# Two-block float32 kernel: the first gate's mixing with the token values stationary, and its row sums as two rounded products

## The chip, the cores and the metric

One core of one Trainium2 chip runs the whole program. The metric is the device time of one execution in microseconds, taken as the median of several runs. The compute engines are TensorE (matrix products, PE in the profile; PEld is its loading of the stationary operand), VectorE (DVE), ScalarE (ACT) and GpSimd (POOL); SyncE (SP) issues most DMAs.

## The reference, cut to what matters

The kernel computes two transformer blocks for 512 tokens of width 1024. The change lies in the spatial gate of the first block (`gmlp_mixer`), with 16 heads of 128 channels and groups of 128 tokens:

```python
u, v, z = jnp.split(h @ w_in, 3, axis=-1)          # each 512 x 2048
u = jax.nn.gelu(u)
v = layer_norm(jax.nn.gelu(v), ln_g, ln_b)
vg = v.reshape(bsz, s // 128, 128, 16, 128)
w_m = jnp.where(allowed[None], w_s, 0)             # per head 128 x 128, s-chunks up to t's
mixed = jnp.einsum('hts,bgshc->bgthc', w_m, vg)
mixed = mixed + b_s.T[:, :, None]
y = u * mixed.reshape(bsz, s, 2048) * jax.nn.silu(z)
return y @ w_out
```

The layer norm's gain `ln_g` and shift `ln_b` are per channel, so the kernel applies them behind the mixing: mixed = ln_g * (W n) + ln_b * (row sums of W) + b_s, where n is the normalised v without gain and shift.

## The kernel before

All matrix products are made of float32 operands split into two rounded parts (`hi`, and `lo` = value - `hi`, type fp32r): a product is `mm3`, three TensorE products hi*hi, lo*hi and hi*lo (L499 to L501) that accumulate in PSUM. Every weight comes in slabs of 128x1024 in one global order: SyncE loads a slab into `raw`, ScalarE rounds it into `whi` (a "cut", L1079), GpSimd subtracts to get `wlo` (L489), and TensorE uses it; the ring has four places, so the cut of a slab waits until TensorE has used the slab four places before. `slab()` is one slab on TensorE: 8 x 3 products of 512 columns into one PSUM bank.

In front of the gate, v has been computed token-major into `vraw` (tokens in partitions, 2048 channels). The gate then runs in eight rounds i, each with two heads q = 0, 1. A round takes four slabs "uz": 4i and 4i+1 give u of the two heads (banks 0 and 1), 4i+2 and 4i+3 give z (banks 2 and 3), all channel-major (channels in partitions, 512 tokens in columns). In round 0 slab 2 comes ahead of the mixing. Beside that, in each round:

- VectorE normalises the round's 256 channels of `vraw` (`norm`, L1629), ScalarE rounds them into `vhi` (L1140) and VectorE makes `vlo` (L1633). ScalarE rounds the two heads' mixing matrices `wt` (s in partitions, t in columns, 128x128 each) into `wthi` (L1143), and VectorE makes `wtlo` (L1636).
- TensorE sums the columns of `wt` over the partitions with a float32 product with `ones` into bank 3 (`rows`, L586, between slabs 4i and 4i+1), and VectorE makes of it the two heads' rows of `bb` = ln_b * rows + b_s (L1641).
- After slab 4i+1 TensorE mixes: `mm3` with `wthi`/`wtlo` stationary and the values moving, 512 columns, into bank 4+q (`mix`, L596). The result is token-major. ScalarE copies it to `mt` (`mixed`, L1157), TensorE transposes it in four 128x128 pieces into bank 6+q (`turn`, L607), after slab 4i+2 for q = 0 and after slab 4i+3 for q = 1.
- VectorE makes mt = ln_g * turned + bb (`affine`, L1647), times gelu(u) (`gate`, L1654), times silu(z) (`y`, L1657), and splits it into `yhi`, `ylo` (L1660, L1662), first all for q = 0, then all for q = 1. ScalarE makes gelu(u) (`u0`, `u1`, L1146, L1153) and silu(z) (`z0`, `z1`, L1159, L1161).

Each engine executes its own list in order. Between engines the order is set by semaphores, counted by `Steps`: `X.at("name", i)` is the count at which step "name" of round i is done. VectorE's list in a round is norm, vlo, wlo, bb, then affine, gate, y, yhi, ylo for q = 0 and for q = 1; norm of round i+1 waits for ylo1 of round i. ScalarE's is cut, vhi, whi, cut, u0, two small loads of the next `wt`, cut, u1, mixed0, mixed1, cut, z0, z1. Behind the gate the output projection `w1` begins.

## Time and profile before

| | |
|---|---|
| median of 3 runs | 1323.53 us (1321.55 to 1324.12) |
| profiled execution, time | 1324.05 us |
| its span, first to last instruction | 1322.3 us |
| TensorE busy | 1303.1 us (99%), 6515 products |
| VectorE busy | 728.6 us (55%) |
| ScalarE busy | 664.7 us (50%) |
| GpSimd busy | 497.0 us (38%) |
| mean granted TensorE clock | 0.994 of full speed |

A timeline gives for each instruction its start and length in us from the start of the span. TensorE's products are pipelined: one is recorded from its start to its last result, and the next starts before that, so cost is read from the distance between starts. A row with "x4" merges four instructions, from the first start to the last end. In brackets stands how long the engine was idle before it, and what released it. "L586" is a line of the kernel.

### The profile page before, as it was taken

How to read it: one execution, taken by the hardware profiler on the slowest of the kernel's cores; microseconds unless marked ns; L12 is line 12 of the kernel's file. 1: busy time of each engine (PE TensorE's matmuls, PEld its weight loads, DVE VectorE, ACT ScalarE, POOL GpSimd, SP SyncE). 2: the span in 40 equal slices, each digit the busy share in tenths (PEclk: the TensorE clock that was granted, in tenths of full speed). 3: DMA queues.
4: the chain of work that ended last, by engine and by line, in shares of the span. 5: the costliest groups of instructions: out<-in, count | busy, mean ns of one | idle time of the engine just before them, and what ended most of it. 6: DMA issues, size and time to landing. Idle time of an engine off the chain costs nothing.

```text
span 1322.3 us, 16669 instructions
## 1 busy us (share of the span) xinstructions
PE 1303.1 (99%) x6515; PEld 1089.8 (82%) x6515; DVE 728.6 (55%) x1288; ACT 664.7 (50%) x999; POOL 497.0 (38%) x207
## 2 busy tenths in 40 slices
PE   9999999999999999999999999999999999999997
PEld 7888888888887788888878888888878888888896
DVE  5556466462137465565865467666645556643444
ACT  5535444443234567575547566656545545552321
POOL 4543433434444322321436433433333333334520
PEclk9999999999999999999999999999999999999998
DMA  5732322324333222322243322222223222235411
GB/s 182 266 119 83 102 84 83 102 83 160 96 111 96 82 92 71 113 68 63 84 154 110 96 65 65 79 80 64 80 81 98 75 81 84 86 106 173 153 39 65
DMA packets 43455, 131.31 MB, mean 99 GB/s; under 512 B 7088, under 2 KB 11888, under 8 KB 42864
## 3 DMA queue, kind: packets, MB, share of 16 engines
q1 hardware_dynamic: 38144, 116.41, 28.5%
q10 hardware_dynamic: 5232, 13.83, 3.0%
q8 instruction: 52, 0.85, 0.3%
q14 instruction: 27, 0.22, 0.1%
HBM read 123.92 MB, written 10.49 MB: 102 GB/s over the span
## 4 chain that ended last, share of the span: by engine, by line
PE 80%; DVE 10%; ACT 6%; issue 2%; DMA 1%; POOL 1%; SPq 0%; DVEq 0%; ACTq 0%
PE banks L499 24%; PE banks L501 24%; PE banks L500 24%; PE banks L685 2%; DVE hd L1899 1%; PE banks L677 1%; PE banks L666 1%; DMA raw<-w 1%; DVE naccb L1804 1%; DVE ylo L1701 1%; ACT L1344 1%; ACT L1343 1%; PE banks L910 1%; PE banks L791 1%; DVE nfull L1697 1%
## 5 line engine op out<-in xcount | busy, mean ns | idle before, releaser
L489 POOL TENSOR_TENSOR wlo<-raw,whi 128x1024 fp32r<-128x1024 f32 (+2 forms) x198 | 486.0, 2456 | 744.8 <-ACT whi L1079 744.5
L499 PE MATMUL banks<-hhi,whi 128*128 128x512 f32 x752 | 307.0, 408 | 2.4 <-DVE hlo L1831 1.2
L501 PE MATMUL banks<-hlo,whi 128*128 128x512 f32 x752 | 294.7, 392 | 0.0
L500 PE MATMUL banks<-hhi,wlo 128*128 128x512 f32 x752 | 294.1, 391 | 0.0
L1079 ACT ACTIVATE whi<-raw 128x1024 fp32r<-128x1024 f32 (+2 forms) x198 | 205.6, 1039 | 173.5 <-PE banks L501 109.4
L499 PE MATMUL banks<-yhi,whi 128*128 128x512 f32 x448 | 176.9, 395 | 0.2 <-DVE ylo L1701 0.2
L501 PE MATMUL banks<-ylo,whi 128*128 128x512 f32 x448 | 174.7, 390 | 0.0
L500 PE MATMUL banks<-yhi,wlo 128*128 128x512 f32 x448 | 174.4, 389 | 0.0
L499 PEld LDWEIGHTS banks<-hhi,whi 128*128 128x128 f32 x752 | 142.0, 189 | 32.1 <-issue 3.1
L501 PEld LDWEIGHTS banks<-hlo,whi 128*128 128x128 f32 x752 | 141.4, 188 | 30.7
L500 PEld LDWEIGHTS banks<-hhi,wlo 128*128 128x128 f32 x752 | 142.1, 189 | 27.1 <-issue 2.2
L499 PEld LDWEIGHTS banks<-yhi,whi 128*128 128x128 f32 x448 | 84.1, 188 | 20.9 <-issue 3.2
L501 PEld LDWEIGHTS banks<-ylo,whi 128*128 128x128 f32 x448 | 84.1, 188 | 18.0
L500 PEld LDWEIGHTS banks<-yhi,wlo 128*128 128x128 f32 x448 | 84.1, 188 | 17.3 <-issue 0.2
L499 PE MATMUL banks<-whi,yhi 128*128 128x512 f32 x224 | 89.3, 399 | 0.7 <-DVE ylo L1559 0.7
L500 PE MATMUL banks<-whi,ylo 128*128 128x512 f32 x224 | 87.9, 392 | 0.0
L501 PE MATMUL banks<-wlo,yhi 128*128 128x512 f32 x224 | 87.8, 392 | 0.0
L499 PEld LDWEIGHTS banks<-whi,yhi 128*128 128x128 f32 x224 | 42.4, 189 | 11.6 <-issue 1.4
L1647 DVE SCALAR_TENSOR_TENSOR mt<-banks,vec,bb 128x512 f32<-128x512 f32 x16 | 12.0, 751 | 70.2 <-PE banks L607 70.2
L500 PEld LDWEIGHTS banks<-whi,ylo 128*128 128x128 f32 x224 | 42.4, 189 | 9.0 <-issue 0.5
L501 PEld LDWEIGHTS banks<-wlo,yhi 128*128 128x128 f32 x224 | 42.5, 190 | 8.9
L1216 ACT ACTIVATE sc<-sc,sm 128x128 f32<-128x128 f32 (+1 forms) x64 | 35.2, 552 | 27.5 <-DVE sm L1759 27.5
(385 smaller groups left out, 2212.9 us busy)
## 6 DMA issues: line engine op xcount, KB each, us to landing
raw<-w SPq DMA_DIRECT2D x193, 512.0 KB, 3.6
rel_tab<-relx ACTq DMA_DIRECT2D x1, 4096.0 KB, 20.3
tab<-rel_tab SPq DMA_DIRECT2D x16, 224.0 KB, 3.5
x<-xt ACTq DMA_DIRECT2D x1, 2048.0 KB, 9.4
x_kept<-x ACTq DMA_DIRECT2D x1, 2048.0 KB, 7.3
parts_kept<-mcg SPq DMA_DIRECT2D x8, 256.0 KB, 4.4
mgt<-parts_kept SPq DMA_DIRECT2D x8, 256.0 KB, 4.1
x<-x_kept ACTq DMA_DIRECT2D x1, 2048.0 KB, 7.9
```

The lines of the kernel that those rows point to most:

```text
L489: nc.gpsimd.tensor_tensor(lo[:, begin:width], raw[:, n % 2, begin:width], f32(hi[:, begin:width]), ALU.subtract).then_inc(lo_done, 1)
L499: nc.tensor.matmul(dst, a[0], b[0], start=first, stop=False)
L500: nc.tensor.matmul(dst, a[1], b[0], start=False, stop=False)
L501: return nc.tensor.matmul(dst, a[0], b[1], start=False, stop=last)
L666: done = nc.tensor.matmul(banks[:, c:c + QW[t]], a[rows, t * P:(t + 1) * P], b[rows, 0:QW[t]], start=first, stop=last)
L677: last = nc.tensor.transpose(banks[:, c:c + P], sc[:, q, of:of + P], ident)
L685: last = nc.tensor.matmul(bank[AO[i][q]][:, k * P:S], av[q][:, i, k, :], p[:, q, AK[q][k]:AK[q][k] + KW[k]], start=k == 0 and p is phi, st ...
L791: nc.tensor.matmul(bank[6], ones, ho[:, 0, :], start=True, stop=True).then_inc(hoP.did("ms"), 1)
L910: last = nc.tensor.transpose(bank[b][:, c:c + P], msc[:, QO[t] + k * P:QO[t] + (k + 1) * P], ident)
L1079: nc.scalar.activation(parts(slab)[0][:, begin:width], raw[:, n % 2, begin:width], ACT.Copy).then_inc(hi_done, 1)
L1216: e = nc.scalar.activation(row, row, ACT.Exp, bias=sm[:, q, 1, t:t + 1], accum_out=sm[:, q, 2, t:t + 1])
L1343: nc.scalar.activation(he[:, :], bank[0], ACT.Sigmoid).then_inc(hpA.did("f"), 1)
```

## The change

Mixing is turned round. The stationary operand is now a 128x128 tile of the values (`vhi` or `vlo`; tokens of one tile t by the channels of head q), and the moving one is the head's matrix: the two parts of it lie side by side in one tile `wts[:, q, g, :]` (g = 0 hi, g = 1 lo). For each head and token tile there are two products: `vhi` with both parts (256 columns, start), and `vlo` with the hi part (128 columns), which accumulates onto the first half. The result is channel-major, so nothing is transposed. It lies in two PSUM banks per head (`mixes[q]`), with vhi*hi + vlo*hi in half 0 and vhi*lo in half 1 of each token tile. ScalarE copies half 1, times ln_g, to `mt` (`mixed`), VectorE adds ln_g times half 0 (`affine`), and a further VectorE step adds `bb` (`shift`).

The row sums are now two products of 256 columns with a rounded `rones` stationary, over the hi and over the lo parts of the two heads. They stand behind slab 4i+1 and behind the wait for `wlo`, directly ahead of the mixing. `rones` is made once by VectorE. ScalarE no longer waits for `rows` ahead of the loads of the next `wt`, and TensorE no longer waits for these loads itself.

```diff
--- before.py
+++ after.py
@@ -203,8 +203,8 @@
             vhi = sb("vhi", [P, TT, 2 * P], F32R, scope)
             vlo = sb("vlo", [P, TT, 2 * P], F32R, scope)
             wt = sb("wt", [P, 2, P], F32, scope)
-            wthi = sb("wthi", [P, 2, P], F32R, scope)
-            wtlo = sb("wtlo", [P, 2, P], F32R, scope)
+            wts = sb("wts", [P, 2, 2, P], F32R, scope)
+            rones = sb("rones", [P, P], F32R, scope)
             mt = sb("mt", [P, 2, S], F32, scope)
             ug = sb("ug", [P, 2, S], F32, scope)
             sz = sb("sz", [P, 2, S], F32, scope)
@@ -285,6 +285,7 @@
 
         banks = ctx.enter_context(nc.psum_tensor("banks", [P, 8 * S], F32))
         bank = [banks[:, i * S:(i + 1) * S] for i in range(8)]
+        mixes = [banks[:, (4 + 2 * q) * S:(6 + 2 * q) * S].rearrange("p (t g v) -> p t g v", t=TT, v=P) for q in range(2)]
 
 
 
@@ -339,11 +340,11 @@
         vA = steps("v_act", numbered("gelu", TT), 4)
         vV = steps("v_dve", numbered("stats", TT), 4)
         vaA = steps("va_act", ["root"])
-        vaV = steps("va_dve", ["mask", "aggr", "eps", "inv", "shift"])
-        uzP = steps("uz_pe", ["rows", "mix0", "mix1", "turn0", "turn1"], 8, prime=1)
+        vaV = steps("va_dve", ["mask", "ones", "aggr", "eps", "inv", "shift"])
+        uzP = steps("uz_pe", ["rows", "mix0", "mix1"], 8, prime=1)
         uzA = steps("uz_act", ["vhi", "whi", "u0", "u1", "mixed0", "mixed1", "z0", "z1"], 8, prime=1)
         uzV = steps("uz_dve", ["norm", "vlo", "wlo", "bb"] + [f"{n}{q}" for q in range(2)
-                    for n in ("affine", "gate", "y", "yhi", "ylo")], 8, prime=1)
+                    for n in ("affine", "shift", "gate", "y", "yhi", "ylo")], 8, prime=1)
         w1A = steps("w1_act", ["sq", "hi"], KT)
         w1V = steps("w1_dve", ["x", "acc", "lo"], KT)
         avP = steps("av_pe", numbered("v", TT - 1), 2)
@@ -578,35 +579,30 @@
                     pe.wait_ge(vA.sem, vA.at(f"gelu{TT - 1}", 2))
                 pe.wait_ge(uzA.sem, uzA.at("u0", i - 1))
                 slab("uz", 4 * i, bank[0], h)
-                pe.wait_ge(uzA.sem, uzA.at("z1", i - 1))
-                pe.wait_ge(ld_wt, 32 * i + 32)
-                if i == 0:
-                    pe.wait_ge(vaV.sem, vaV.at("mask"))
-                    pe.wait_ge(vA.sem, vA.at(f"gelu{TT - 1}", 2))
-                nc.tensor.matmul(bank[3][:, 0:2 * P], ones, wt[:, :, :], start=True, stop=True).then_inc(uzP.did("rows"), 1)
                 pe.wait_ge(uzA.sem, uzA.at("u1", i - 1))
                 slab("uz", 4 * i + 1, bank[1], h)
                 if i == 0:
                     slab("uz", 2, bank[2], h)
                     pe.wait_ge(vA.sem, vA.all())
                 pe.wait_ge(uzV.sem, uzV.at("wlo", i))
+                pe.wait_ge(uzA.sem, uzA.at("z1", i - 1))
+                for g in range(2):
+                    rows = nc.tensor.matmul(bank[3][:, 0:2 * P], rones[:, :], wts[:, :, g, :], start=g == 0, stop=g == 1)
+                rows.then_inc(uzP.did("rows"), 1)
                 for q in range(2):
-                    pe.wait_ge(uzA.sem, uzA.at(f"mixed{q}", i - 1))
+                    pe.wait_ge(uzV.sem, uzV.at(f"affine{q}", i - 1))
                     cols = slice(q * P, (q + 1) * P)
-                    mm3(bank[4 + q][:, :], (wthi[:, q, :], wtlo[:, q, :]), (vhi[:, :, cols], vlo[:, :, cols]),
-                        True, True).then_inc(uzP.did(f"mix{q}"), 1)
+                    for t in range(TT):
+                        nc.tensor.matmul(mixes[q][:, t, :, :], vhi[:, t, cols], wts[:, q, :, :], start=True, stop=False)
+                        mix = nc.tensor.matmul(mixes[q][:, t, 0, :], vlo[:, t, cols], wts[:, q, 0, :], start=False,
+                                               stop=True)
+                    mix.then_inc(uzP.did(f"mix{q}"), 1)
                 for q in range(2):
                     if i or q:
                         pe.wait_ge(uzA.sem, uzA.at(f"z{q}", i - 1))
                         if q == 1:
                             pe.wait_ge(uzV.sem, uzV.at("bb", i))
                         slab("uz", 4 * i + 2 + q, bank[2 + q], h)
-                    pe.wait_ge(uzA.sem, uzA.at(f"mixed{q}", i))
-                    pe.wait_ge(uzV.sem, uzV.at(f"affine{q}", i - 1))
-                    for t in range(TT):
-                        turn = nc.tensor.transpose(bank[6 + q][:, t * P:(t + 1) * P], mt[:, q, t * P:(t + 1) * P],
-                                                   ident)
-                    turn.then_inc(uzP.did(f"turn{q}"), 1)
 
 
             pe.wait_ge(uzA.sem, uzA.at("u0", 7))
@@ -1140,12 +1136,11 @@
                 nc.scalar.activation(vhi[:, :, :], vraw[:, :, bass.ds(i * 2 * P, 2 * P)],
                                      ACT.Copy).then_inc(uzA.did("vhi"), 1)
                 act.wait_ge(ld_wt, 32 * i + 32)
-                nc.scalar.activation(wthi[:, :, :], wt[:, :, :], ACT.Copy).then_inc(uzA.did("whi"), 1)
+                nc.scalar.activation(wts[:, :, 0, :], wt[:, :, :], ACT.Copy).then_inc(uzA.did("whi"), 1)
                 cut()
                 act.wait_ge(uzV.sem, uzV.at("gate0", i - 1))
                 nc.scalar.activation(ug[:, 0, :], bank[0][:, :], ACT.Gelu_apprx_tanh).then_inc(uzA.did("u0"), 1)
                 act.wait_ge(uzV.sem, uzV.at("wlo", i))
-                act.wait_ge(uzP.sem, uzP.at("rows", i))
                 act.dma_start(wt[0:64, :, :], ws[0:64, bass.ds(2 * i + 2, 2), :]).then_inc(ld_wt, 16)
                 act.dma_start(wt[64:P, :, 64:P], ws[64:P, bass.ds(2 * i + 2, 2), 64:P]).then_inc(ld_wt, 16)
                 cut()
@@ -1154,7 +1149,8 @@
                 for q in range(2):
                     act.wait_ge(uzP.sem, uzP.at(f"mix{q}", i))
                     act.wait_ge(uzV.sem, uzV.at(f"ylo{q}", i - 1))
-                    nc.scalar.activation(mt[:, q, :], bank[4 + q][:, :], ACT.Copy).then_inc(uzA.did(f"mixed{q}"), 1)
+                    nc.scalar.activation(mt[:, q, :].rearrange("p (t v) -> p t v", v=P), mixes[q][:, :, 1, :], ACT.Copy,
+                                         scale=col("ln_g", 2 * i + q)).then_inc(uzA.did(f"mixed{q}"), 1)
                 cut()
                 nc.scalar.activation(sz[:, 0, :], bank[2][:, :], ACT.Silu).then_inc(uzA.did("z0"), 1)
                 used("uz", 4 * i + 3)
@@ -1608,6 +1604,7 @@
                 if k in (2, 6):
                     stats_of(1 if k == 2 else 2)
             stats_of(3)
+            V.tensor_copy(rones[:, :], ones).then_inc(vaV.did("ones"), 1)
             dve.wait_ge(vV.sem, vV.all())
             for t in range(TT):
                 last = V.bn_aggr(mv[:, t, :], stats[:, t, :, :])
@@ -1633,7 +1630,7 @@
                 V.tensor_tensor(vlo[:, :, :], vraw[:, :, bass.ds(i * 2 * P, 2 * P)], f32(vhi[:, :, :]),
                                 ALU.subtract).then_inc(uzV.did("vlo"), 1)
                 dve.wait_ge(uzA.sem, uzA.at("whi", i))
-                V.tensor_tensor(wtlo[:, :, :], wt[:, :, :], f32(wthi[:, :, :]), ALU.subtract).then_inc(uzV.did("wlo"), 1)
+                V.tensor_tensor(wts[:, :, 1, :], wt[:, :, :], f32(wts[:, :, 0, :]), ALU.subtract).then_inc(uzV.did("wlo"), 1)
                 if i == 0:
                     dve.wait_ge(ld_bs, 16)
                 dve.wait_ge(uzP.sem, uzP.at("rows", i))
@@ -1643,13 +1640,14 @@
                 last.then_inc(uzV.did("bb"), 1)
                 dve.wait_ge(uzV.sem, uzV.at("bb", i))
                 for q in range(2):
-                    dve.wait_ge(uzP.sem, uzP.at(f"turn{q}", i))
-                    V.scalar_tensor_tensor(mt[:, q, :].rearrange("p (t v) -> p t v", v=P),
-                                           bank[6 + q][:, :].rearrange("p (t v) -> p t v", v=P),
-                                           col("ln_g", 2 * i + q),
-                                           bb[:, bass.ds(2 * i + q, 1), :].to_broadcast([P, TT, P]),
-                                           ALU.mult, ALU.add).then_inc(uzV.did(f"affine{q}"), 1)
+                    dve.wait_ge(uzA.sem, uzA.at(f"mixed{q}", i))
+                    mt3 = mt[:, q, :].rearrange("p (t v) -> p t v", v=P)
+                    V.scalar_tensor_tensor(mt3, mixes[q][:, :, 0, :], col("ln_g", 2 * i + q), mt3, ALU.mult,
+                                           ALU.add).then_inc(uzV.did(f"affine{q}"), 1)
                     dve.wait_ge(uzV.sem, uzV.at(f"affine{q}", i))
+                    V.tensor_tensor(mt3, mt3, bb[:, bass.ds(2 * i + q, 1), :].to_broadcast([P, TT, P]),
+                                    ALU.add).then_inc(uzV.did(f"shift{q}"), 1)
+                    dve.wait_ge(uzV.sem, uzV.at(f"shift{q}", i))
                     dve.wait_ge(uzA.sem, uzA.at(f"u{q}", i))
                     V.tensor_tensor(mt[:, q, :], mt[:, q, :], ug[:, q, :], ALU.mult).then_inc(uzV.did(f"gate{q}"), 1)
                     dve.wait_ge(uzV.sem, uzV.at(f"gate{q}", i))
```

## Rows read from the trace of the kernel before

**Rows 1.** The page: busy time of each engine, and the chain that ended last.

```profile
PE 1303.1 (99%) x6515; PEld 1089.8 (82%) x6515; DVE 728.6 (55%) x1288; ACT 664.7 (50%) x999; POOL 497.0 (38%) x207
...
PE 80%; DVE 10%; ACT 6%; issue 2%; DMA 1%; POOL 1%; SPq 0%; DVEq 0%; ACTq 0%
```

**Rows 2.** Work by stretch (us, then busy us of each engine, clock, DMA): the first gate.

```profile
97.65:294.90 197.25, 197.25 (x898) 162.53 (x897) 112.58 (x150) 93.53 (x118) 79.92 (x32) 1.00 0.30 91
```

**Rows 3.** TensorE's timeline (start us, length us), round 3 of the gate.

```profile
201.76 0.60 PE L586 MATMUL banks<-wt,cst 128*128 128x256 f32 x2
...
202.43 0.39 PE L500 MATMUL banks<-hhi,wlo 128*128 128x512 f32 x1
...
207.68 0.40 PE L499 MATMUL banks<-vhi,wthi 128*128 128x512 f32 x1
...
209.07 0.39 PE L499 MATMUL banks<-hhi,whi 128*128 128x512 f32 x1
...
214.56 0.60 PE L607 MATMUL banks<-cst,mt 128*128 128x128 f32 x4
...
215.22 0.39 PE L500 MATMUL banks<-hhi,wlo 128*128 128x512 f32 x1
...
220.46 0.60 PE L607 MATMUL banks<-cst,mt 128*128 128x128 f32 x4
...
232.29 0.40 PE L499 MATMUL banks<-vhi,wthi 128*128 128x512 f32 x1
```

**Rows 4.** TensorE's timeline, first and last of 23 products, 256 columns.

```profile
1011.06 0.28 PE L500 MATMUL banks<-whi,llo 128*128 128x256 f32 x1
...
1013.70 0.28 PE L501 MATMUL banks<-wlo,lhi 128*128 128x256 f32 x1
```

**Rows 5.** TensorE's timeline, second block: 128-column products, then one of 512.

```profile
732.67 0.22 PE L499 MATMUL banks<-hqxhi,hkhi 128*128 128x128 f32 x1
...
733.57 0.39 PE L500 MATMUL banks<-hhi,wlo 128*128 128x512 f32 x1
```

**Rows 6.** TensorE's timeline, round 0 of the gate.

```profile
115.61 0.40 PE L501 MATMUL banks<-vlo,wthi 128*128 128x512 f32 x1
116.01 0.66 PE L607 MATMUL banks<-cst,mt 128*128 128x128 f32 x4
```

**Rows 7.** VectorE's timeline: rounds 0 and 3, then behind the gate.

```profile
108.41 0.42 DVE L1636 TENSOR_TENSOR wtlo<-wt,wthi 128x256 fp32r<-128x256 f32 x1
...
117.56 0.69 DVE L1654 TENSOR_TENSOR mt<-mt,ug 128x512 f32<-128x512 f32 x1
...
215.26 0.75 DVE L1647 SCALAR_TENSOR_TENSOR mt<-banks,vec,bb 128x512 f32<-128x512 f32 x1 [8.62 <-PE banks L607]
216.05 2.85 DVE L1654 TENSOR_TENSOR mt<-mt,ug 128x512 f32<-128x512 f32 x1
...
222.61 2.77 DVE L1657 TENSOR_TENSOR mt<-mt,sz 128x512 f32<-128x512 f32 x1
...
230.33 0.42 DVE L1636 TENSOR_TENSOR wtlo<-wt,wthi 128x256 fp32r<-128x256 f32 x1
230.66 0.61 DVE L1641 SCALAR_TENSOR_TENSOR bb<-banks,vec,bb 128x128 f32<-128x128 f32 x2
...
307.81 0.69 DVE L1673 TENSOR_TENSOR x<-x,banks 128x512 f32<-128x512 f32 x1 [9.22 <-DMA x<-xt]
```

**Rows 8.** GpSimd's timeline, round 3 and the start of round 4.

```profile
215.96 2.40 POOL L489 TENSOR_TENSOR wlo<-raw,whi 128x1024 fp32r<-128x1024 f32 x1 [4.46 <-ACT whi L1079]
222.29 2.54 POOL L489 TENSOR_TENSOR wlo<-raw,whi 128x1024 fp32r<-128x1024 f32 x1 [3.94 <-ACT whi L1079]
230.41 2.60 POOL L489 TENSOR_TENSOR wlo<-raw,whi 128x1024 fp32r<-128x1024 f32 x1 [5.58 <-ACT whi L1079]
```

**Rows 9.** ScalarE's timeline, round 3: the first silu.

```profile
217.19 0.60 ACT L1159 ACTIVATE sz<-banks 128x512 f32<-128x512 f32 x1
```

**Rows 10.** GpSimd's timeline, round 0.

```profile
117.67 2.84 POOL L489 TENSOR_TENSOR wlo<-raw,whi 128x1024 fp32r<-128x1024 f32 x1 [3.36 <-ACT whi L1079]
```

## What the change will do to the time

> **What bounds the kernel now.** I read the page first. TensorE is busy for 1303.1 of 1322.3 us, and the chain that ended last is 80% TensorE work [rows 1]. That alone says little, since a busy share is an average over stages, so I then read the three stretches: before, inside and after the first gate. In the gate (97.65 to 294.90 us, the eight rounds that the change edits) TensorE is busy for 197.25 of 197.25 us, while VectorE has 112.6, ScalarE 93.5 and GpSimd 79.9 us of work; the granted clock is 1.00, the upper of the two levels (2.4 GHz) [rows 2]. So in this stretch time is what TensorE has to issue, and every us taken from it is worth a us, as long as nothing else becomes late. The reader should see both halves: the sum of TensorE's work, and the slack of the chain that feeds it.
>
> For the sum I don't take durations, which overlap (a 512-column product lasts 0.39 us, yet the next starts 0.23 us later), but distances between starts, in one steady round (round 3) of TensorE's timeline [rows 3].
>
> **What TensorE loses, per round.** The row sum over `ones` (L586, float32, two passes): from its start at 201.76 to 202.43, the second product after it, is 0.67, less one usual distance of 0.23, so 0.44 us. Mixing: six products of 512 columns, 207.68 to 209.07, 1.39 us. Transposes: four at 214.56, and 215.22 - 214.56 - 0.23 = 0.43 us; the group at 220.46 is its twin, so 0.86 us. Together 2.69 us [rows 3].
>
> **What TensorE gains, per round.** Rows: two rounded products of 256 columns. Back-to-back products of that width and type stand 2.64 us apart over 22 steps, 0.120 us each [rows 4], so 0.24 us. Mixing: for each of two heads and four token tiles one product of 256 columns and one of 128. For 128 columns the trace has the hgrn products: six of them from 732.67, then wide ones, of which the second starts at 733.57; 0.90 less 0.23 is 0.67 us, 0.111 each [rows 5]. One pair thus costs 0.231 and eight pairs 1.85 us. I take 0.120 after the wide one and 0.111 after the narrow one because each distance is measured in a series of its own width; no row shows them alternating. Bounds: both at 0.111 give 1.78 us, both at 0.120 give 1.92 us. The columns streamed are the same as before (6x512 = 8x384 = 3072), so the stationary reloads cost 0.46 us per round, and what is won is the transposes and the cheaper row sum. New total 2.09 us, a gain of 0.60 us per round (0.53 to 0.67), 4.8 us in eight rounds (4.2 to 5.4).
>
> A rule that would change this term: the Trainium skill, TensorE: Matmul & The Clock Gate, section Back-to-back issue gap, gives the isolated distance at the full clock as N/2.4 + 2.5 ns, that is 56 ns for 128 columns. An estimate by that page makes new mixing 8x(0.109+0.056) = 1.32 us and the total gain some 4 us larger. The row of 0.111 us disagrees, so I price by the row; the same page's LDWEIGHTS section (128 columns, about 107 ns) agrees with the row.
>
> One idle piece goes as well: in round 0 TensorE's last mixing product starts at 115.61, its successor could start at 115.84, and the transposes start at 116.01 because they wait for ScalarE's copy [rows 6]. That is 0.17 us, once. The new order has no such wait; what stands in its place is `bb`, which slab 3 waits for. `bb` starts after `rows`, which is now ahead of 1.85 us of mixing, and takes 0.61 us of VectorE [rows 7]: covered.
>
> **What moves, and who waits.** The rows' product moves from behind slab 4i to behind slab 4i+1, and now waits for `wlo` and, with it, the mixing. Queued behind it on TensorE is everything. So the question is whether `wlo` still comes in time. ScalarE loses its wait on `rows` ahead of the two small `wt` loads; that wait was long over, and both loads are issued from the same place. VectorE's `bb` is later by one slab (5.49 us), but VectorE then sat idle for 8.62 us waiting for the transposes [rows 7], so nothing queues behind it that matters. ScalarE's copy out of PSUM gets a scale and a strided source; even at twice its time it is hidden, since what it starts (affine0, shift0, gate0) is done some 5 us before z0, which y0 needs as well. One extra 128x128 copy (`rones`) lies in VectorE's prologue, where `wlo` of round 0 ends at 108.83 [rows 7] and the last of six mixing products starts at 115.61 [rows 6], so some 5 us are free; without that cover it would cost 0.2 us once.
>
> **The chain that feeds TensorE.** It is z1 and y0, then affine1, gate1, y1, yhi1, ylo1, norm, vhi, vlo, `wlo`. Measured from the end of slab 4i+3 (220.46, where the twin of the transposes starts): `wlo` ends at 230.33 + 0.42 = 230.75 [rows 7], 10.29 us later; mixing starts at 232.29 [rows 3], 11.83 later. Slack 1.54 us. After the change TensorE asks for `rows` after two slabs only, 2 x 5.49 = 10.98 us, and VectorE has one more instruction per head, `shift`, a 128x512 sum of two SBUF tensors (0.69 us, like the gate at 117.56 [rows 7]). Naively 10.29 + 0.72 = 11.01 and the slack is gone. But the row to look at is y1 itself: 2.77 us instead of 0.69, from 222.61 to 225.38. GpSimd runs its split from 222.29 to 224.83 [rows 7, 8]. Gate0 shows the same (2.85 us, ending 218.90, 0.54 after GpSimd's 218.36). VectorE's sums of two SBUF tensors stand still while GpSimd works, and end 0.54 us after it. Y1's end is pinned to GpSimd, and part of the new instruction fits in the time it stood.
>
> The Trainium skill, SBUF — State Buffer, section SBUF: two separate sides, states this as an exclusive lock: whichever of a two-SBUF-input VectorE instruction and a GpSimd instruction starts first holds it to its end. The trace agrees.
>
> Worked through in the clock of round 3 (slab 4i+2 ends at 214.56): mixing no longer waits for transposes, so affine0, shift0 and gate0 run early, shift0 behind a GpSimd split, done some 5 us after `rows`, far ahead of z0 (217.19 + 0.60 = 217.79 [rows 9]). Y0 then stands until 218.90; yhi0 and ylo0 end at 220.09, affine1 (0.75) at 220.88, shift1 at 221.61, gate1 runs 221.64 to 222.33. Slab 4i+3 ends at 214.56 + 5.49 = 220.05 and GpSimd's split asks 1.83 us later (222.29 - 220.46), at 221.88, 0.24 after gate1 began. It then ends 2.26 us after the VectorE instruction that held it up, as at 117.67 + 2.84 = 120.51 against 117.56 + 0.69 [rows 7, 10], at 224.59, and y1 at 225.13: 5.08 after the slab, where it was 4.92. So `wlo` is done 10.45 us after the slab and TensorE asks at 10.98. Slack 0.53 us, no stall. If gate1 loses the race, y1 ends at 225.54, `wlo` at 10.86: still in time. Round 0 is out of step (no slab 2 between mixing and slab 3): there ylo0 ends near 122.2, shift1 holds off GpSimd, gate1 stands behind it, and `wlo` of round 1 ends 132.6 against a request at 132.6: a stall of 0.1 us, 0.7 if shift1 loses.
>
> **The sum.** 4.8 + 0.17 - 0.1 = 4.9 us. Behind the gate all is paced by TensorE or relative to it; the load of `x`, issued when ylo1 of round 7 is done, lands for 307.81 [rows 7], and TensorE needs that sum four slabs after 294.7, at 316.7, so it is hidden as before. The profiled execution took 1324.05 us (span 1322.3), so 1319.2; it stood 0.5 above the median of the three runs, so the median would be 1318.7. I say 1319.0.
>
> **Rivals.** (A) VectorE's chain becomes the bound. If shift1 loses to GpSimd too (needs affine1 0.95 us later than worked out), `wlo` comes 10.86 + 0.72 = 11.58 after the slab, 0.60 us late in seven rounds, 4.2 us: 1323.4, no change. For: slack falls from 1.54 to 0.53 us. Against: the pin to GpSimd. Chance 0.10. (B) Slower: `wlo` starts at 230.33, GpSimd's next split at 230.41 [rows 7, 8], 0.08 us apart. Should the split start first, in every round, because ScalarE's `whi` into the interleaved tile is that much quicker or `vlo` later, `wlo` ends near 230.41 + 2.40 + 0.27 = 233.08, about 12.8 us after the slab with the 0.16 from above, 1.8 us late seven times: 1324.05 - 5.0 + 12.6 = 1331.7. It decides at 0.08 us. Against: both hang on the same `vhi`, and the eight pairs of the eight rounds all stand 0.08 to 0.10 apart. Chance 0.06. (C) A narrow product costs its columns only. From 0.229 us for 512 (5.49 over 24) and 0.120 for 256 columns [rows 3, 4], a straight line gives 0.066 for 128: a pair 0.186, mixing 1.49 us, 8 x 0.36 = 2.9 us more gain, 1316.3. Against: the series at 0.111 [rows 5], though in it every product is narrow and reloads follow each other at once, where here a wide one stands between. Chance 0.04; it is the side to which the page's formula points. The forecast has 0.80.
>
> **Numbers.** A measurement of this kernel can tell about 0.2% (2.6 us) from no change. Low end: best bounds 5.4 + 0.17 off 1324.05 give 1318.5, less 0.5 for the median and 1.7 for scatter (the runs shown spread 2.6): 1316.3, which takes in C as well. High end takes in A, 1323.4. B stays out, with the tails of the rest. Forecast and C are faster (0.83 after a little for scatter), A is within 0.2%, some of it with B: same 0.11, slower 0.06.
>
> **What the profile after would show.** No transposes; products of 256 and 128 columns with starts 0.120 and 0.111 apart; a round of 24.0 us instead of 24.62; TensorE without idle time in the gate except at most 0.1 us ahead of `rows` of round 1; shift0 near 3 us long, shift1 0.69; y1 ending about 5.1 us after slab 4i+3; `wlo` 0.42 long ending 0.5 us before `rows`. What would make me wrong: TensorE waiting for `wlo` in each round (A for 0.6, B for 1.8 us with a long `wlo`), or other distances between the short products.

## The result, and the profile after

The changed kernel took 1314.7 us in the median of five runs (1314.39 to 1315.8), the kernel before 1323.53 beside it (1321.53 to 1324.48): ratio 0.994, 95% interval 0.9928 to 0.9952. It is faster by 8.8 us, where 4.5 to 4.9 were forecast; 1314.7 lies 1.6 us under the low end of the range. Two later series of the same two kernels gave 1315.59 against 1322.94 (0.9939) and 1315.45 against 1323.62 (0.994). The profiled execution took 1314.39 us, span 1312.6.

The page of the kernel after (busy time of each engine; chain that ended last), beside [rows 1]:

```profile
PE 1295.1 (99%) x6531; PEld 1087.0 (83%) x6531; DVE 729.9 (56%) x1305; ACT 664.4 (51%) x999; POOL 496.0 (38%) x207
...
PE 80%; DVE 11%; ACT 6%; issue 2%; POOL 0%; DMA 0%; DVEq 0%; SPq 0%; ACTq 0%
```

Nothing changed its role. To find where 9.7 us of span went I cut both spans at the same events: the first column sum behind the gate's projection, the second group of mean squares, what follows it, and TensorE's last products. Windows of the kernel before (us; busy us of PE, PEld, DVE, ACT, POOL; granted clock; DMA share; GB/s), then of the kernel after:

```profile
384.50:674.30 289.80, 287.13 (x1496) 238.54 (x1494) 179.47 (x397) 172.88 (x301) 99.16 (x41) 1.00 0.29 91
674.30:682.30 8.00, 8.00 (x33) 6.60 (x34) 1.70 (x7) 1.16 (x2) 2.39 (x1) 0.79 0.42 147
682.30:1314.50 632.20, 625.20 (x3288) 530.59 (x3287) 356.92 (x640) 324.77 (x484) 229.59 (x93) 1.00 0.28 87
1314.50:1322.30 7.80, 0.67 (x2) 0.00 (x0) 3.22 (x8) 0.00 (x0) 0.00 (x0) 0.50 0.41 136
```

```profile
97.65:290.00 192.35, 192.30 (x919) 161.74 (x918) 113.73 (x168) 94.26 (x118) 80.06 (x32) 1.00 0.32 94
...
378.50:668.30 289.80, 287.10 (x1496) 238.55 (x1494) 179.43 (x397) 172.63 (x301) 99.17 (x41) 1.00 0.30 91
668.30:674.70 6.40, 6.40 (x34) 5.47 (x34) 1.71 (x7) 1.16 (x2) 2.39 (x1) 1.00 0.38 153
674.70:1306.10 631.40, 625.00 (x3288) 530.43 (x3287) 358.01 (x640) 324.37 (x484) 228.99 (x93) 1.00 0.29 88
1306.10:1312.60 6.50, 0.41 (x2) 0.00 (x1) 3.22 (x8) 0.00 (x0) 0.00 (x0) 0.54 0.49 161
```

The reader should see separate pieces. Up to the column sum the kernel after is 6.0 us ahead (384.5 against 378.5). Over the next 290 us the two differ by some 0.02 us. Then 1.6 us come in a stretch of 8 us where the clock column reads 0.79 against 1.00, 0.8 us over the long rest, and 1.3 us in the last 8 us. So 3.7 us of the 9.7 lie where nothing was edited. The 0.8 us lie within the scatter: the same rest takes 632.2 and 633.0 us in the two profiles of the kernel before, and 631.4, 632.5 and 632.6 in the three of the kernel after.

The time in front of the gate is no constant either, so the edited part is best measured between two events of its own: the gate's first product and the column sum. TensorE's timeline, kernel before, then after:

```profile
97.65 0.39 PE L499 MATMUL banks<-hhi,whi 128*128 128x512 f32 x1
...
384.53 0.61 PE L649 MATMUL banks<-cst,nacc 128*128 128x1 f32 x5
```

```profile
97.56 0.39 PE L500 MATMUL banks<-hhi,whi 128*128 128x512 f32 x1
...
378.53 0.61 PE L645 MATMUL banks<-cst,nacc 128*128 128x1 f32 x5
```

That is 286.88 against 280.97 us, a gain of 5.9. Every profile of either kernel gives these two lengths within 0.01 us; "later" and "earlier" below are differences between such lengths.

In the gate, TensorE's timeline of round 3 of the kernel after (start us, length us), beside [rows 3]:

```profile
204.20 0.40 PE L590 MATMUL banks<-wts,rones 128*128 128x256 f32 x2
204.44 0.28 PE L596 MATMUL banks<-wts,vhi 128*128 128x256 f32 x1
204.56 0.22 PE L597 MATMUL banks<-wts,vlo 128*128 128x128 f32 x1
204.62 0.33 PE L596 MATMUL banks<-wts,vhi 128*128 128x256 f32 x1
204.79 0.22 PE L597 MATMUL banks<-wts,vlo 128*128 128x128 f32 x1
...
206.24 0.44 PE L500 MATMUL banks<-hhi,whi 128*128 128x512 f32 x1
206.52 0.40 PE L501 MATMUL banks<-hhi,wlo 128*128 128x512 f32 x1
...
228.06 0.40 PE L590 MATMUL banks<-wts,rones 128*128 128x256 f32 x2
```

From the rows to the second wide product, less one distance: 206.52 - 204.20 - 0.23 = 2.09 us, as forecast. A pair (204.79 less 204.56) is 0.23, but not split as forecast: 0.06 us pass from the narrow product to the wide one behind it (204.62) and 0.17 from that to the next. The round, though, is 228.06 - 204.20 = 23.86 us, where 24.0 was forecast. The kernel before has its next row sum at 226.37, a round of 24.61:

```profile
226.37 0.60 PE L586 MATMUL banks<-wt,cst 128*128 128x256 f32 x2
```

Take the short work away from both: 24.61 - 2.69 = 21.92 us for the four slabs of a round before, 23.86 - 2.09 = 21.77 after. The same 96 wide products cost 0.2283 us each before and 0.2268 after. That is 0.15 us a round, 1.2 us in eight.

The chain that feeds TensorE, in VectorE's timeline of the kernel after, and GpSimd's beside it:

```profile
208.09 1.07 DVE L1648 TENSOR_TENSOR mt<-mt,bb 128x512 f32<-128x512 f32 x1
...
218.69 0.69 DVE L1652 TENSOR_TENSOR mt<-mt,ug 128x512 f32<-128x512 f32 x1
219.42 2.77 DVE L1655 TENSOR_TENSOR mt<-mt,sz 128x512 f32<-128x512 f32 x1
...
227.13 0.42 DVE L1633 TENSOR_TENSOR wts<-wt,wts 128x256 fp32r<-128x256 f32 x1
```

```profile
219.00 2.62 POOL L490 TENSOR_TENSOR wlo<-raw,whi 128x1024 fp32r<-128x1024 f32 x1 [3.47 <-ACT whi L1075]
227.22 2.58 POOL L490 TENSOR_TENSOR wlo<-raw,whi 128x1024 fp32r<-128x1024 f32 x1 [5.59 <-ACT whi L1075]
```

Gate1 starts ahead of GpSimd's split (218.69 against 219.00), y1 is stretched and ends at 222.19, and `wlo` ends at 227.55, 0.51 us ahead of the rows at 228.06. Forecast was 0.53.

### The profile page after: what moved, and what is told of

The parts are those of the page before. It is cut to its first block, busy times and chain, and to the rows that moved or that the text cites. A ratio compares the mean times of both kernels' runs of the same rounds, so it can differ in the third digit from the quotient of the medians.

```text
span 1312.6 us, 16685 instructions
## 1 busy us (share of the span) xinstructions
PE 1295.1 (99%) x6531; PEld 1087.0 (83%) x6531; DVE 729.9 (56%) x1305; ACT 664.4 (51%) x999; POOL 496.0 (38%) x207
## 4 chain that ended last, share of the span: by engine, by line
PE 80%; DVE 11%; ACT 6%; issue 2%; POOL 0%; DMA 0%; DVEq 0%; SPq 0%; ACTq 0%
PE banks L500 24%; PE banks L502 24%; PE banks L501 24%; PE banks L681 2%; DVE hd L1897 1%; PE banks L673 1%; PE banks L662 1%; DVE naccb L1802 1%; DVE ylo L1699 1%; PE banks L596 1%; ACT L1340 1%; ACT L1339 1%; PE banks L906 1%; PE banks L787 1%; DVE hb L1894 1%
## 5 line engine op out<-in xcount | busy, mean ns | idle before, releaser
L1655 DVE TENSOR_TENSOR mt<-mt,sz 128x512 f32<-128x512 f32 x16 | 26.3, 1642 | 37.8 <-ACT sz L1155 37.5
```

The lines of the kernel that those rows point to most:

```text
L1655: V.tensor_tensor(mt[:, q, :], mt[:, q, :], sz[:, q, :], ALU.mult).then_inc(uzV.did(f"y{q}"), 1)
```

## The experiments

**Both kernels again.** The spread and the landmarks have to be known before parts are compared.

> The kernel before, unchanged: how far one execution stands from another. The gate (first product at 97.65, first of the column-wise sums behind the output projection at 384.5) should repeat within 0.2 us. Theory G (the difference between the two profiled executions is 6.0 us in the gate and the rest is which level the clock happened to be at): the stretch at 1.2 GHz that the first profile had behind the mean squares (675 to 679 us, 1.5 us lost) is there in some executions and not in others, and the span varies by 1 to 3 us. Theory R (the rest of the gain belongs to the change): the stretch is there again at the same place, and the median stays near 1323.5.

> The changed kernel, unchanged. Theory G: the gate repeats (sums behind the projection at 378.5), and the stretch behind the mean squares may be at 1.2 GHz this time, which costs 1.5 us; over many executions the mean difference to before should come out nearer to 6 to 7 us than to 9. Theory R: no low clock there, difference 8.8 again.

Measured: before 1323.04 us (0.9998, 0.9989 to 1.0007), column sum at 384.4; after 1315.59 (0.9939, 0.9926 to 0.9953), column sum at 378.4. So the 6.0 us come back to a tenth. I also counted in the two traces, up to the column sum, the wide products whose distance to the next is above 0.2285 us ("slow" from here on), and summed their excess over 0.2267: 249 and 1.43 us before, 23 and 0.10 us after. The 1.6 us behind the mean squares don't come back: this profile of the kernel before has the full clock there and a span of 1321.2.

**The parts of the gate.** The new rows alone, in the kernel before:

```diff
-                nc.tensor.matmul(bank[3][:, 0:2 * P], ones, wt[:, :, :], start=True, stop=True).then_inc(uzP.did("rows"), 1)
...
+                for g, part in enumerate((wthi, wtlo)):
+                    rows = nc.tensor.matmul(bank[3][:, 0:2 * P], rones[:, :], part[:, :, :], start=g == 0, stop=g == 1)
```

> The kernel before with the row sums alone changed (two rounded products directly ahead of the mixing; mixing and transposes as before). By the prediction's prices the sums behind the projection come 8 x 0.20 = 1.6 us earlier (at 382.9). Theory S (each interruption of a series of 512-column products makes the next 5 to 16 of them slower, 0.227 to 0.231 us): 8 x 0.04 more, 1.9 us, and 512-column products slower than 0.2285 us fall from 240 to about 170 in the gate. Time 1321.6 to 1321.9.

Measured: 1318.45 us (0.9968, 0.9955 to 0.998), column sum at 382.3, 2.1 us earlier, and 168 slow products (0.96 us) in place of 249. A round is 24.36 us, 0.25 shorter where the prices give 0.20.

The kernel before without its transposes:

```diff
-                    for t in range(TT):
-                        turn = nc.tensor.transpose(bank[6 + q][:, t * P:(t + 1) * P], mt[:, q, t * P:(t + 1) * P],
-                                                   ident)
...
-                                           bank[6 + q][:, :].rearrange("p (t v) -> p t v", v=P),
+                                           bank[4 + q][:, :].rearrange("p (t v) -> p t v", v=P),
```

> The kernel before without the transposes: the affine step reads the token-major mixing result as if it were channel-major, so this part of the result is not computed as in the reference. By the prediction's prices 8 x 0.86 + 0.17 = 7.05 us less up to the sums behind the projection (377.5). Theory S: another 8 x 0.045, 7.4 us (377.1), and some 80 slow 512-column products fewer in the gate. The chain to wlo gets no longer than before plus nothing, as no shift step is added: TensorE is not idle in the gate.

Measured: 1315.57 us (0.9944, 0.9932 to 0.9957), 170 slow products (1.00 us). The column sum is at 377.4, which looks like 7.0 us, just what the prices alone give. But TensorE had waited 1.1 us for a cut of ScalarE's in front of the gate, where the kernels do not differ, and the gate began late. Its first product and the column sum:

```profile
98.21 0.39 PE L499 MATMUL banks<-hhi,whi 128*128 128x512 f32 x1
...
377.41 0.61 PE L643 MATMUL banks<-cst,nacc 128*128 128x1 f32 x5
```

That is 279.20 us, 7.7 less than before; theory S had 7.4. A round is 23.68 us, 0.93 shorter where the prices give 0.86.

The changed kernel with the float32 row sum back in its old place:

```diff
+                nc.tensor.matmul(bank[3][:, 0:2 * P], ones, wt[:, :, :], start=True, stop=True).then_inc(uzP.did("rows"), 1)
...
-                for g in range(2):
-                    rows = nc.tensor.matmul(bank[3][:, 0:2 * P], rones[:, :], wts[:, :, g, :], start=g == 0, stop=g == 1)
```

> The changed kernel with the row sums undone (float32 product at its old place between slabs 4i and 4i+1, mixing new). By the prices: the sums behind the projection 1.6 us later than in the changed kernel (380.1). Theory S: 1.6 + 8 x 0.04 = 1.9 us later (380.4), with 9 slow 512-column products behind each of the eight.

Measured: 1317.63 us (0.9964, 0.9951 to 0.9977), column sum at 380.2, 1.7 us later than after, between the 1.6 of the prices and the 1.9 of theory S; 86 slow products (0.48 us). By the counts the float32 row sum leaves 8 to 10 slow products behind it each time ((249 - 168)/8, (86 - 24)/8), a group of four transposes about 5 ((249 - 170)/16), and old mixing about 11 (the rest, 249 - 81 - 79 = 89 in eight rounds), five of its own six among them (the six took 1.39/6 = 0.232 us each). The new mixing and rows leave at most 3 a round.

**Interruptions elsewhere.** Four products of 128 columns ahead of a slab in six rounds of the projection behind the gate, in the changed kernel, once as float32 transposes and once on rounded operands:

```diff
+                if m >= 2:
+                    for t in range(TT):
+                        nc.tensor.transpose(bank[5][:, t * P:(t + 1) * P], ident, ident)
```

```diff
+                if m >= 2:
+                    for t in range(TT):
+                        nc.tensor.matmul(bank[5][:, t * P:(t + 1) * P], yhi[:, 0, 0:P], yhi[:, 0, 0:P], start=True, stop=True)
```

> The changed kernel with four extra 128x128 float32 transposes of the identity into an unused bank in each of six output-projection rounds (between the two slabs, m from 2): 24 in all, nothing else. Own cost 6 x 0.43 = 2.6 us. Theory S: five or more slow 512-column products behind each group, 6 x 0.025 = 0.15 us more; in the changed kernel this stretch has 3 slow ones, here it should have over 30.

> The changed kernel with four products of 128 columns on rounded (fp32r) operands in each of the last six projection rounds, where the run with four float32 transposes there (e8) came out at the column sum behind the projection 3.0 us later than the changed kernel and with 37 more slow 512-column products (0.23 us). Here the four cost 4 x 0.056 to 4 x 0.111 us a round (the narrow product of a wide and narrow pair, at most), 1.3 to 2.7 us in all. Theory F (only float32 products leave slow 512-column products behind them): the number of slow products stays near the changed kernel's 24 (0.09 us); column sum at 379.8 to 381.1. Theory I (any interruption of the stream does): 30 to 40 slow products more and 0.2 us, column sum at 380.0 to 381.4. The count tells them apart, the time does not.

Measured: transposes 1319.69 us (0.9982, 0.9973 to 0.9991), column sum at 381.5, 2.9 us later, 61 slow products (0.34 us): 6 a group. Rounded products 1319.23 us (0.9964, 0.995 to 0.9977), column sum at 381.4, 2.8 us later, 33 slow products (0.15 us): 1.5 a group. So the count went theory F's way; the time did not, 381.4 being later than F's 381.1. TensorE's timeline of the rounded ones shows why:

```profile
338.79 0.56 PE L619 MATMUL banks<-yhi 128*128 128x128 f32 x4
339.19 0.45 PE L500 MATMUL banks<-yhi,whi 128*128 128x512 f32 x1
339.47 0.40 PE L501 MATMUL banks<-yhi,wlo 128*128 128x512 f32 x1
```

The four take 339.19 - 338.79 = 0.40 us, but the wide product behind them is followed after 0.28 us instead of 0.23, 0.45 us in all, six times 2.7. Old mixing ran on rounded operands too and was slow, so "float32 only" is not the whole rule: a group of short rounded products is cheap to interrupt with, a float32 group is not. What in the engine makes the next five to ten products 2 to 9 ns late stays open.

**How much slack the chain has.** One, then two more sums of two SBUF tensors between shift1 and gate1 of each round, in the changed kernel:

```diff
+                    if q == 1:
+                        V.tensor_tensor(spare[:, :], ug[:, q, :], sz[:, 0, :], ALU.add).then_inc(uzV.did("more0"), 1)
```

> The changed kernel with one more 128x512 sum of two SBUF tensors per round on VectorE, into a spare tile, between shift1 and gate1 (0.72 us with its start). The slack of the chain to wlo is 0.51 us in the changed kernel. Naive theory (each VectorE instruction counts in full): wlo 0.2 us late in seven rounds, 1.5 us. Theory P (y1 is pinned to the end of GpSimd's split): the extra sum holds the split off or gate1 stands behind it; y1 ends at most 0.4 us later, no more than 0.1 us idle in a round beyond round 1, time within 0.5 us of the changed kernel.

> Two such sums (1.44 us). Naive theory: wlo 0.93 us late in seven rounds, 6.5 us. Theory P: the first 0.7 us vanish against GpSimd's split; one sum is held up by it and what is behind comes after: 0.5 to 0.7 us idle ahead of the rows' product in seven rounds, 3.5 to 4.9 us slower than the changed kernel.

Measured: one sum 1318.07 us (0.9965, 0.9953 to 0.9978), column sum at 381.5, 3.0 us later; two 1322.65 us (1.0001, 0.9991 to 1.001), at 385.9, 7.2 us later. Theory P had 0.5 us at most and 3.5 to 4.9, the naive one 1.5 and 6.5, so the idea of the prediction that time in this chain is hidden behind y1's pin to GpSimd falls. VectorE's timeline with one sum more:

```profile
220.56 0.69 DVE L1654 TENSOR_TENSOR spare<-ug,sz 128x512 f32<-128x512 f32 x1
221.16 2.88 DVE L1655 TENSOR_TENSOR mt<-mt,ug 128x512 f32<-128x512 f32 x1
224.08 0.69 DVE L1658 TENSOR_TENSOR mt<-mt,sz 128x512 f32<-128x512 f32 x1
```

Now gate1 is the one that stands while GpSimd works, and y1 runs behind it in 0.69: one stretched instruction has taken the other's place and everything behind is 0.72 us later. TensorE's timeline with one sum (first fence) and with two:

```profile
205.43 0.39 PE L503 MATMUL banks<-hlo,whi 128*128 128x512 f32 x1
205.92 0.50 PE L591 MATMUL banks<-wts,rones 128*128 128x256 f32 x2
206.26 0.28 PE L597 MATMUL banks<-wts,vhi 128*128 128x256 f32 x1
```

```profile
207.45 0.39 PE L503 MATMUL banks<-hlo,whi 128*128 128x512 f32 x1
208.55 0.50 PE L591 MATMUL banks<-wts,rones 128*128 128x256 f32 x2 [0.71 <-DVE wts L1634]
```

The rows come 0.49 and 1.10 us after the last wide product, where 0.23 is usual: 0.26 and 0.87 us of waiting, for 0.72 and 1.44 us of added work. So the slack was 0.46 to 0.57 us, which is what the timeline showed (0.51), and the naive theory has the waits right (0.2 and 0.93). A wait costs more than its length: the rows then take 0.34 us instead of 0.24, and with some more slow products behind them (43 in the trace with one sum, against 23) a steady round loses 0.41 us instead of 0.26.

**The end of the kernel.** A window over the last DMA issues, kernel before and then after (packets of each queue; last line: issues and median us to landing):

```profile
q1 hardware_dynamic: 345, 0.30, 32.4%
q14 instruction: 1, 0.01, 0.7%
...
out<-x SPq DMA_DIRECT2D x1, 128.0 KB, 2.8
```

```profile
q1 hardware_dynamic: 647, 0.58, 60.5%
...
out<-x SPq DMA_DIRECT2D x3, 128.0 KB, 1.8
```

In the kernel before a load of instructions (8 KB, queue q14) starts 2.16 us ahead of the end of the span, in the midst of the last output packets. All but 15 of these have started by 1.75 us ahead of the end; those 15 follow one at a time until 0.85 us ahead of it. From VectorE's last end to the end of the span it is 3.8 us there and 2.8 in the kernel after, whose load starts 14.4 us ahead of the end. Every kernel with the small copy into `rones` has the short end, every one without it the long one. So I added that tile and its copy to the kernel before, and the tile alone:

```diff
+            rones = sb("rones", [P, P], F32R, scope)
...
+            V.tensor_copy(rones[:, :], ones).then_inc(vaV.did("ones"), 1)
```

> The kernel before with one addition, the tile of rounded ones and the one VectorE copy that fills it, which nothing reads. Every profile of a kernel without that copy (before, its repeat, the one without transposes) has an 8 KB instruction load on queue q14 2.2 to 2.3 us ahead of the end of the span, the last output DMA taking 2.8 us to land, and 3.7 to 3.8 us from VectorE's last end to the end of the span; every profile with the copy has that load 11 us or more ahead of the end, a landing of 1.8 us and 2.8 us from VectorE's end. Theory L (where the instruction load falls depends on how many instructions VectorE has in its program, and it holds up one DMA engine at the end): with the copy the load moves away from the end, the last landing is 1.8 us, VectorE's end to the span's end 2.8 us, and the median is 0.9 to 1.1 us below the kernel before: 1321.6 to 1322.1; the gate is unchanged (column sum behind the projection at 384.4 to 384.6, some 249 slow products). Rival N (the short tail comes from something else that the new rows or the new mixing bring): the load stays 2.2 us ahead of the end, the tail is 3.8 us, the median 1322.5 to 1323.1.

> The kernel before with the tile of rounded ones declared and nothing done with it: the tiles behind it in the gate's part of the memory shift by 512 bytes per partition, no instruction is added. Theory L (the count of VectorE's instructions places the load): nothing changes, load 2.2 to 2.4 us ahead of the end, tail 3.7 to 3.8 us, median 1322.5 to 1323.1. Rival M (the layout of the memory shortens the tail): tail 2.8 us, median 1321.6 to 1322.1. If the slow 512-column products hung on the layout too, their number in the gate would fall from some 249; by what they follow it stays.

Measured: with the copy 1321.98 us (0.9989, 0.9981 to 0.9998), with the tile alone 1322.78 (0.9999, 0.999 to 1.0008). The same window of the two, copy first:

```profile
q1 hardware_dynamic: 654, 0.59, 61.2%
...
out<-x SPq DMA_DIRECT2D x3, 128.0 KB, 1.8
```

```profile
q14 instruction: 1, 0.01, 1.0%
...
out<-x SPq DMA_DIRECT2D x1, 128.0 KB, 2.6
```

With the copy the load has moved to 11.6 us ahead of the end, and the tail is 2.8 us; with the tile alone it is at 2.25 us and the tail is 3.6. Both gates are unchanged (249 slow products, column sum at 384.6 and 384.3). One instruction more in VectorE's program thus takes about a microsecond off the end (0.8 us between the two medians, 1.3 against the kernel before, interval of the latter 0.3 to 2.5), in a place that has nothing to do with it. Theory L's forecast came. The other profiles agree: the load starts 2.2 to 2.3 us ahead of the end in all four with 1288 VectorE instructions, 11.2 and 11.6 in the two with 1289, 14.1 to 14.9 in the six with 1305, 17.5 with 1313 (one sum more) and 23.5 with 1321 (two), whether TensorE has 6451 or 6555 products. So its place follows VectorE's number of instructions. That it holds up one DMA engine fits the rows but was not shown.

**The clock.** The 1.6 us behind the mean squares:

> The changed kernel once more, for the share of the gain that the granted clock has. Of 58 runs of the kernel before, 17 had a mean granted clock of 0.994 (mean 1323.9 us), 16 of 0.995 (1322.9), 22 of 0.996 (1322.15) and 3 of 0.997; of the 10 runs of the changed kernel so far, one had 0.995 and nine 0.996 or 0.997 (eight at 0.996, mean 1315.1 us). At equal clock the gain is 7.0 us, which is 6.0 us of the gate and 1.0 us of the last landing; what the medians show above that would be the clock. Theory K (the changed kernel falls to the lower clock less often): at least 8 in 10 of the runs at 0.996 or more, median 1314.5 to 1315.6. Rival Z (it was the draw of ten runs): about half of the runs at 0.994 or 0.995, median 1315.6 to 1316.5, and the gain over the kernel before 7.0 us or a little more.

Measured: 1315.45 us (0.994, 0.9926 to 0.9953); mean clocks 0.996 four times and 0.997 once, where six of the nine runs of the kernel before beside it had 0.994 or 0.995. With the earlier ones that is 14 of 15 runs of the changed kernel at 0.996 or more, and 28 of 67 of the kernel before. Theory K holds as an observation. TensorE's timeline of the kernel before shows what one such stretch is:

```profile
673.38 1.02 PE L751 MATMUL banks<-cst,nacc 128*128 128x1 f32 x8 [0.30 <-DVE naccb L1804]
674.27 1.03 PE L751 MATMUL banks<-cst,naccb 128*128 128x1 f32 x8
675.16 0.65 PE L499 MATMUL banks<-whi,yhi 128*128 128x512 f32 x1
675.61 0.63 PE L500 MATMUL banks<-whi,ylo 128*128 128x512 f32 x1
676.03 0.63 PE L501 MATMUL banks<-wlo,yhi 128*128 128x512 f32 x1
```

Behind sixteen products of one column, from 675.3 to 678.7, wide products last 0.63 us and start 0.43 apart: the granted clock is at its lower level (1.2 GHz) and costs 1.6 us. In the profiles of the kernel after, three in all, the same sixteen products are followed by the upper level. Of the kernel before one has it and one hasn't. But four variants of the changed kernel have it in their profiles (the old row sum, one and two more sums, the added transposes), and with the added transposes 6 of 10 runs had a mean clock of 0.994 or 0.995. So the runs don't tie the upper level to the change itself. Why the changed kernel falls less often is open; two identical executions can differ in it. This third profile of the kernel after has its column sum at 379.1, 0.6 us later than the first, all of it from in front of the gate (first product at 98.11); its gate is as long as the others'.

## Why the prediction was wrong

**TensorE bounds the gate**: right. 192.30 of 192.35 us busy, as [rows 2].

**Removed 2.69, added 2.09 us per round**: right to a hundredth, but in the sum only. The distances inside a pair were 0.17 and 0.06 us and not the 0.120 and 0.111 that the prediction said the profile would show. The narrow product handed on after 0.06 us, a quarter of the 0.227 of 512 columns, and the wide one took the difference back. The prediction had said that no row shows the two alternating; that its sum held to a hundredth is in part luck. The pair cost 0.231 and not 0.186, so rival C's gain did not come. The isolated distance that the Trainium skill gives (TensorE: Matmul & The Clock Gate, section Back-to-back issue gap), 56 ns for 128 columns, fits the narrow product's 0.06 us; as a price of the pair (0.165 us, an estimate by that page) it does not.

**"Slab 5.49 us", the step that failed inside the gate.** I read a slab's length once, [rows 3], with its slow products in it, and held it constant. It is no constant: it carries the after-effect of what interrupts the stream. Taking away the float32 rows, the transposes and old mixing made the 96 wide products of a round 0.15 us shorter: 0.05 by the row sum and 0.07 by the transposes (the rounds of e3 and e4 against the prices), the rest by old mixing. The term was missing from the sum and measured 1.2 us.

**Idle time 0.17 and the stall of 0.1**: the stall of round 1 was longer. TensorE's timeline of the kernel after:

```profile
132.07 0.39 PE L502 MATMUL banks<-hlo,whi 128*128 128x512 f32 x1
132.51 0.51 PE L590 MATMUL banks<-wts,rones 128*128 128x256 f32 x2
132.85 0.29 PE L596 MATMUL banks<-wts,vhi 128*128 128x256 f32 x1
```

The rows come 0.44 us after the last wide product, a stall of 0.21, and take 0.34 instead of 0.24, so this pair comes to 0.17 - 0.31 = -0.14 instead of +0.07. The sum for the gate is 4.8 + 1.2 - 0.14 = 5.9, and 5.9 was measured.

**The chain, rival A and rival B**: the forecast of 0.53 us of slack was right (0.51); neither rival came. `wlo` still starts 0.09 us ahead of the split (B's margin was 0.08). But the reason I gave against A was too good: e6 and e7 show that one instruction more would have brought A's waiting. Shift0 was 1.07 us long and not near 3, as GpSimd's split had begun 1.9 us earlier; nothing hung on it.

**"Behind the gate all is paced by TensorE or relative to it", the second step that failed.** It held for the arithmetic (289.80 us both), not for the instruction load at the end (1.0 us in the profiles) nor for the clock. At an equal mean clock of 0.996 the kernel before averages 1322.2 us (24 runs) and the kernel after 1315.3 (12 runs): 6.9 us, which is the gate's 5.9 and the end's 1.0. What the medians of the three series show above that, 0.5 to 1.9 us, goes with the clock and with scatter; the runs don't separate the two.

So the direction was right and so was what bounds the gate, and 3.9 us of the 8.8 were not in the sum of 4.9: 1.0 in the gate, 1.0 at the end, and 1.9 of clock and scatter. Without these 1.9 the median would have been 1316.6, just inside the range; the range had 1.7 us for scatter, but only on top of the best bounds of the terms that the sum had.

## What to carry to other kernels

Price what interrupts a stream of wide matmuls by the whole round, not by its own distances: here float32 row sums and transposes cost some 8 to 11% more than their own time, in the wide products behind them (0.07 us per 0.86 us of transposes, 0.05 per 0.44 us row sum, from the rounds of e4 and e3). When a gain is read, cut both spans at the same events first, at the start of the edited stage as well as behind it: what happens in front of it moved one reading by 0.7 us. Pieces in stretches that nobody edited have causes of their own, and an otherwise idle copy added to the kernel before shows how large they are. Count slack from the end of the last instruction to its reader, and don't count on a stretched instruction to absorb more work.

## What the runs showed of the hardware

- A 512-column product behind a float32 interruption costs 0.229 to 0.236 us instead of 0.227, for 5 to 10 products; behind four rounded products of 128 columns for one or two.
- TensorE pays about 0.1 us more on its first products after a wait (rows 0.34 us instead of 0.24).
- In an alternation of 256 and 128 columns with a change of operand before each, the starts stand 0.17 and 0.06 us apart, 0.231 a pair.
- With an 8 KB instruction load inside the last output transfer this lands after 2.6 to 2.8 us instead of 1.8; a single added VectorE instruction moved the load from 2.2 to 11.6 us ahead of the end.
- The same program can run a stretch at either clock level from one execution to the next, for 1.6 us a time; runs at a mean clock of 0.994 take 1.75 us more than those at 0.996 (1323.9 against 1322.2, 21 and 24 runs of the kernel before).
